# Stick-breaking stage: VectorE in place of ScalarE copies the turned queries and keys out of the score banks

## The chip, the cores and the metric

One core of one Trainium2 chip runs the whole program in one launch. The metric is the device time of that execution in microseconds. Engines are called as in the profile: PE (TensorE), ACT (ScalarE), DVE (VectorE), POOL (GpSimd), SP (SyncE, which here issues the DMAs).

## The reference

One layer of a decoder for a prompt (16 meta rows and 1024 rows) and 64 sample rows. Branch B, for the prompt, is stick-breaking attention over 8 heads of 64:

```python
z = jnp.einsum('bqhd,blhd->bhql', q, k).astype(jnp.float32) * (HEAD_DIM ** -0.5)
strict = (k_pos[None, :] < q_pos[:, None])[None, None]
log_keep = jnp.where(strict, jax.nn.log_sigmoid(-z), 0.0)
after = lax.cumsum(log_keep, axis=3, reverse=True) - log_keep
log_a = jnp.where(strict, jax.nn.log_sigmoid(z) + after, -jnp.inf)
return jnp.einsum('bhql,blhd->bqhd', jnp.exp(log_a).astype(v.dtype), v)
```

The kernel computes it as sigmoid(z) times a running product, from the right, of sigmoid(-z).

## The kernel before, in words

The program is a row of stages with a barrier between them: norm, projections, index scores, the stick-breaking stage (`stick`, the only one that the change touches, about 728 to 908 us of the span), sparse attention, sample attention, merge, FFN, last norm. Each engine's order of work in `stick` is written out by hand; no scheduler moves anything.

`stick` handles four pairs of heads (i = 0 to 3), and for each pair nine tiles of 128 query rows (t = 0 to 8, the last of 16 rows). Tile t sees (t + 1) x 128 keys, 1040 at most, in chunks of 512. The loop variable n (or g) counts tiles over all pairs, 36 in all.

- PE turns the rows of queries and keys of a pair into columns (`turn_qk`, L1095), in five batches: queries and keys of tiles 0 to 3, queries and keys of tiles 4 to 7, and one of tile 8 with both. It scores a chunk for both heads (`score`, L1107) and adds the mask at the diagonal (L1113), turns the weights of tile n - 3 (`turn`, L1125) and multiplies those of tile n - 4 with the values (`use`, L1143).
- ACT takes two sigmoids of each score chunk (`open_tile`, L1189 into `rest`, L1190 into `prob`), copies the turned weights out (`take_turn`, L1198), and the outputs (`evacuate`, L1207). It also copies the turned queries (L1176, with the scale) and keys (L1179): `take_qk`.
- DVE runs one scan over each head of a tile (L1235), once ACT's last sigmoid of that head and tile is there.
- POOL multiplies `prob` with the shifted scan (L1081).

All of turned queries and keys and score chunks go through four PSUM banks in turn. Each use of a bank is a job; job c uses bank c % 4, and PE may write it only when job c - 4 has been read. The jobs around the step from pair 0 to pair 1 are: tile 6 scores 21 to 24 (two chunks, two heads), batches 25 and 26, tile 7 scores 27 to 30, batches 31 and 32, tile 8 scores 33 to 38, batch 39, tile 0 of the next pair 40 and 41. So the second chunk of tile 7 (29, 30) follows batches 25 and 26 in their banks, and the second chunk of tile 8 (35, 36) follows batches 31 and 32. The batches of the next pair are placed by this table:

```python
QK = [("q", 0, 4), ("k", 0, 4), ("q", 4, 4), ("k", 4, 4), ("both", 8, 1)]
QK_WITH = {6: (0, 1), 7: (2, 3), 8: (4,)}
```

The first scores of a pair wait for all five batches of that pair. SP loads the next pair's rows when PE has turned the last batch of this one.

Of the kernel before, what the change touches and what calls it, by code (L numbers as in the profile page):

```python
# [36 lines left out]
ALU = mybir.AluOpType  # L37
ACT = mybir.ActivationFunctionType
AX = mybir.AxisListType

P = 128
# [933 lines left out]
def stick(nc, ctx, proj, ident, q_rows, k_rows, qk_in, selection, sample_mask, load_ahead, out_t):  # L975
# [8 lines left out]
    def sem(name):  # L984
        return nc.alloc_semaphore(f"st_{name}")
# [3 lines left out]
    QK = [("q", 0, 4), ("k", 0, 4), ("q", 4, 4), ("k", 4, 4), ("both", 8, 1)]  # L989
    QK_WITH = {6: (0, 1), 7: (2, 3), 8: (4,)}  # L990
    TURNS = [(g, hh, k0, min(4, g % NT + 1 - k0)) for g in range(NG) for hh in range(2) for k0 in range(0, g % NT + 1, 4)]
    jobs, scores_of, copies_of = 0, [], {}
    for b in range(len(QK)):
        copies_of[0, b] = jobs
        jobs += 1
    for g in range(NG):
        i, t = divmod(g, NT)
        scores_of.append([])
        for a, w in chunks(key_width(t)):
            for hh in range(2):  # L1000
                scores_of[g].append((jobs, hh, a, w))
                jobs += 1
        for b in QK_WITH.get(t, ()) if i + 1 < PAIRS else ():
            copies_of[i + 1, b] = jobs
            jobs += 1
    turns_of = [[c for c, d in enumerate(TURNS) if d[0] == g] for g in range(NG)]

# [15 lines left out]
    mask_made, mask_stored = sem("mask_made"), sem("mask_stored")  # L1023
    v_in = [sem(f"v_in{b}") for b in range(2)]
    stored = [sem(f"stored{b}") for b in range(2)]
    made, taken, scanned, weighed, turns, turns_out, used, o_out = (
        sem(x) for x in ("made", "taken", "scanned", "weighed", "turns", "turns_out", "used", "o_out"))
    tiled = proj.rearrange("(t p) n -> p t n", p=P)

    def half(hh):  # L1030
# [10 lines left out]
    with nc.Block() as block:  # L1041
# [40 lines left out]

        @block.tensor
        def _(pe):
            def turn_qk(i, b):
                what, t0, n = QK[b]
                c = copies_of[i, b]
                if b == 0:
                    pe.wait_ge(qk_in, 32 * (i + 1))
                if c >= NS:  # L1090
                    pe.wait_ge(taken, c - NS + 1)
                for t in range(t0, t0 + n):
                    for k, rows in enumerate([q_rows, k_rows] if what == "both" else [q_rows if what == "q" else k_rows]):
                        at = (t - t0 + k) * P
                        ins = pe.transpose(banks[c % NS][:, at:at + P], rows[:, t, :], ident[:])  # L1095
                ins.then_inc(made, 1)

            def score(g, k):
                i, t = divmod(g, NT)
                r = tile_rows(t)  # L1100
                if t == 0 and k == 0:
                    pe.wait_ge(taken, copies_of[i, len(QK) - 1] + 1)
                last = scores_of[g][-2][0]
                for c, hh, a, w in scores_of[g][2 * k:2 * k + 2]:
                    if hh == 0:
                        pe.wait_ge(taken, c + 1 - NS + 1)
                    ins = pe.matmul(banks[c % NS][:, 0:w], q_t[i % 2][half(hh), t * P:(t + 1) * P],  # L1107
                                    k_t[i % 2][half(hh), a:a + w], start=True, stop=True)
                    if c < last:
                        ins.then_inc(made, 1)  # L1110
                for c, hh, a, w in scores_of[g][2 * k:2 * k + 2] if 2 * k + 2 == len(scores_of[g]) else ():
                    at = slice(t * P - a, t * P - a + r)
                    pe.matmul(banks[c % NS][0:r, at], spread_one[0:r, 0:r], forbidden[0:r, 0:r], start=False, stop=True,  # L1113
                              skip_group_check=True).then_inc(made, 1)

            def turn(c):
                g, hh, k0, n = TURNS[c]
                r = tile_rows(g % NT)
                pe.wait_ge(weighed, 2 * g + hh + 1)
                if c >= NTB:  # L1120
                    pe.wait_ge(turns_out, c - NTB + 1)
                for j in range(n):
                    kt = k0 + j
                    w = tile_rows(kt)
                    ins = pe.transpose(turned[c % NTB][0:w, j, 0:r], prob[g % R][hh][0:r, kt * P:kt * P + w],  # L1125
                                       ident[0:r, 0:r])
                ins.then_inc(turns, 1)

            def use(g):
                i, t = divmod(g, NT)  # L1130
                r = tile_rows(t)
                if t == 0:
                    pe.wait_ge(v_in[i % 2], 16 * (i // 2 + 1))
                pe.wait_ge(turns_out, turns_of[g][-1] + 1)
                b = i * len(O_GROUPS) + group_of[t]
                first, last = O_GROUPS[group_of[t]]
                at = (t - first) * P
                if t == first and b >= 1:
                    pe.wait_ge(o_out, b)
                for kt in range(t + 1):  # L1140
                    w = tile_rows(kt)
                    for hh in range(2):
                        ins = pe.matmul(o[half(hh), at:at + r], v_rows[i % 2][0:w, kt, half(hh)],  # L1143
                                        prob_t[g % 2][hh][0:w, kt, 0:r], start=kt == 0, stop=kt == t,
                                        skip_group_check=True)
                ins.then_inc(used, 1)

            for b in range(len(QK)):
                turn_qk(0, b)
            pe.wait_ge(mask_made, 3)  # L1150
            for n in range(NG + USE_LAG):
                for k, chunks_beside in woven(n):
                    if k is not None:
                        score(n, k)
                    for c in chunks_beside[:NTB]:
                        turn(c)
                    if not k and n >= USE_LAG:
                        use(n - USE_LAG)
                    for c in chunks_beside[NTB:]:
                        turn(c)  # L1160
                if n < NG:
                    i, t = divmod(n, NT)
                    for b in QK_WITH.get(t, ()) if i + 1 < PAIRS else ():
                        turn_qk(i + 1, b)

        @block.scalar
        def _(act):
            def take_qk(i, b):
                what, t0, n = QK[b]
                c = copies_of[i, b]  # L1170
                act.wait_ge(made, c + 1)
                if b == 0 and i >= 2:
                    act.wait_ge(made, scores_of[(i - 1) * NT - 1][-1][0] + 1)
                at = slice(t0 * P, (t0 + n) * P)
                if what in ("q", "both"):
                    ins = act.activation(q_t[i % 2][:, at], banks[c % NS][:, 0:n * P], ACT.Copy, scale=HD ** -0.5)  # L1176
                if what in ("k", "both"):
                    from_k = P if what == "both" else 0
                    ins = act.activation(k_t[i % 2][:, at], banks[c % NS][:, from_k:from_k + n * P], ACT.Copy)  # L1179
                ins.then_inc(taken, 1)  # L1180

            def open_tile(g, k):
                r = tile_rows(g % NT)
                if g >= R and k == 0:
# [21 lines left out]
                w = min(last * P, NP_ROWS) - first * P  # L1206
                act.activation(o_all[i % 2][:, first * P:first * P + w], o[:, 0:w], ACT.Copy).then_inc(o_out, 1)  # L1207

            for b in range(len(QK)):
                take_qk(0, b)  # L1210
            for n in range(NG + USE_LAG):
                for k, chunks_beside in woven(n):
                    if k is not None:
                        open_tile(n, k)
                    for c in chunks_beside:
                        take_turn(c)
                if n >= USE_LAG:
                    i, t = divmod(n - USE_LAG, NT)
                    if t + 1 == O_GROUPS[group_of[t]][1]:
                        evacuate(i, group_of[t])  # L1220
                if n < NG:
                    i, t = divmod(n, NT)
                    for b in QK_WITH.get(t, ()) if i + 1 < PAIRS else ():
                        take_qk(i + 1, b)

        @block.vector
        def _(dve):
            dve.memset(unread[:], 1.0).then_inc(unread_set, 1)
            dve.wait_ge(unread_set, 1)
            for n in range(NG):  # L1230
                r, w = tile_rows(n % NT), key_width(n % NT)
                for hh in range(2):
                    dve.wait_ge(taken, max(c for c, h2, _, _ in scores_of[n] if h2 == hh) + 1)
                    x = rest[n % R][hh][0:r, 0:w]
                    dve.tensor_tensor_scan(x[:, ::-1], x[:, ::-1], unread[0:r, :].to_broadcast([r, w]), 1.0,  # L1235
                                           ALU.mult, ALU.bypass).then_inc(scanned, 1)


def sparse(nc, ctx, proj, ident, q_rows, k_rows, rows_in, selection, out_t, loads):
# [1473 lines left out]
```

## Time and profile before

| | |
|---|---|
| median of 3 runs | 2368.26 us (2366.24 to 2368.83) |
| profiled execution | 2369.87 us, its span 2368.0 us |
| busy over the span | PE 90%, DVE 59%, ACT 32%, POOL 5% |
| mean granted PE clock | 0.959 |

The busy shares are over all stages. In the rows further down a timeline row gives the start, the length, the engine, the line and the operation, what it writes and reads with its shape, how many such instructions it merges (x), and in brackets how long the engine sat idle before it and what released it. An fp32 matmul appears as two records.

### The profile page before, as it was taken

To read this page: it belongs to the slowest core of one execution; us is meant where nothing else is said; L and a number is where in the kernel's file an instruction comes from. 1 tells how busy PE (TensorE), PEld (TensorE's weight loads), DVE (VectorE), ACT (ScalarE), POOL (GpSimd) and SP (SyncE) were. 2 spreads that over 40 slices of the span, in tenths; PEclk is the share of its full clock that TensorE was granted. 3 is DMA by queue.
4 is the path that set the end of the run, shared out by engine and by line. 5 is a ranking of instruction groups with operands and counts; after the bars stand their busy time and mean duration, and the time that the engine had idled before them with its cause. 6 is when DMAs were issued, how large, how long until landed. Compare 5 with 4: busy or idle time off the path is not lost. (4 is left out here: it accounts for less than half of the span.)

```text
span 2368.0 us, 36885 instructions
## 1 busy us (share of the span) xinstructions
PE 2129.3 (90%) x13337; PEld 1768.3 (75%) x13337; DVE 1385.3 (59%) x2428; ACT 764.9 (32%) x1433; POOL 110.3 (5%) x120
## 2 busy tenths in 40 slices
PE   4876999999998987887886989799999999999995
PEld 4832888888885655555555878699999999999994
DVE  5448967665594565573434453345656656656556
ACT  4046011111216896673334331222212122122122
POOL 0000000000004451001000000000000000000000
PEclk7988999999999999998998999899999999999997
DMA  4321222223223102632998440021111011011102
GB/s 152 99 46 45 101 85 85 85 90 114 85 70 94 47 24 65 189 127 81 332 366 316 139 166 27 12 64 54 35 44 53 27 53 53 27 53 36 43 21 89
DMA packets 186052, 218.73 MB, mean 92 GB/s; under 512 B 28828, under 2 KB 119324, under 8 KB 184796
## 3 DMA queue, kind: packets, MB, share of 16 engines
q1 hardware_dynamic: 185300, 217.20, 28.0%
q8 instruction: 65, 1.06, 0.2%
q14 instruction: 39, 0.32, 0.0%
q10 hardware_dynamic: 648, 0.15, 0.0%
HBM read 181.17 MB, written 36.13 MB: 92 GB/s over the span
## 5 line engine op out<-in xcount | busy, mean ns | idle before, releaser
L2447 DVE TENSOR_TENSOR x_all<-x_all,ff_down 128x512 f32<-128x512 f32 x396 | 269.9, 688 | 159.3 <-PE ff_down L2351 159.1
L2336 PE MATMUL ff_up<-m_hi,ff_up_hi 128*128 128x368 f32 x1056 | 348.2, 330 | 8.8 <-DVE ff_up_lo L2424 8.8
L2337 PE MATMUL ff_up<-m_lo,ff_up_hi 128*128 128x368 f32 x1056 | 349.0, 330 | 0.0
L2338 PE MATMUL ff_up<-m_hi,ff_up_lo 128*128 128x368 f32 x1056 | 347.2, 329 | 0.0
L419 PE MATMUL pr_acc<-pr_w_hi,h_hi 128*128 128x512 f32 x720 | 281.0, 390 | 16.3 <-DVE pr_w_lo L356 16.3
L420 PE MATMUL pr_acc<-pr_w_lo,h_hi 128*128 128x512 f32 x720 | 280.7, 390 | 0.0
L421 PE MATMUL pr_acc<-pr_w_hi,h_lo 128*128 128x512 f32 x720 | 280.6, 390 | 0.0
L819 DVE TENSOR_SCALAR_CACHE_REDUCE bi_flags<-scores,bi_thr 128x384 bf16<-128x384 f32 (+6 forms) x231 | 215.9, 993 | 1.2
L2336 PEld LDWEIGHTS ff_up<-m_hi,ff_up_hi 128*128 128x128 f32 x1056 | 198.7, 188 | 10.0 <-DVE ff_up_lo L2424 9.2
L2337 PEld LDWEIGHTS ff_up<-m_lo,ff_up_hi 128*128 128x128 f32 x1056 | 198.7, 188 | 0.8
L2338 PEld LDWEIGHTS ff_up<-m_hi,ff_up_lo 128*128 128x128 f32 x1056 | 198.8, 188 | 0.0
L339 ACT ACTIVATE pr_staged<-pr_acc 128x512 f32<-128x512 f32 x72 | 43.1, 599 | 399.0 <-PE pr_acc L421 399.0
L419 PEld LDWEIGHTS pr_acc<-pr_w_hi,h_hi 128*128 128x128 f32 x720 | 135.6, 188 | 44.6 <-DVE pr_w_lo L356 16.4
L2349 PE MATMUL ff_down<-ff_down_hi,ff_g_hi 128*128 128x512 f32 x396 | 155.1, 392 | 5.8 <-issue 5.8
L421 PEld LDWEIGHTS pr_acc<-pr_w_hi,h_lo 128*128 128x128 f32 x720 | 135.6, 188 | 28.2
L420 PEld LDWEIGHTS pr_acc<-pr_w_lo,h_hi 128*128 128x128 f32 x720 | 135.6, 188 | 28.0
L2351 PE MATMUL ff_down<-ff_down_hi,ff_g_lo 128*128 128x512 f32 x396 | 155.2, 392 | 0.0
L2350 PE MATMUL ff_down<-ff_down_lo,ff_g_hi 128*128 128x512 f32 x396 | 155.1, 392 | 0.0
L1235 DVE TENSOR_TENSOR_SCAN st_rest<-st_rest,st_unread 128x128 f32<-128x128 f32 (+8 forms) x72 | 100.8, 1444 | 67.3 <-ACT st_prob L1190 67.2
L2378 ACT ACTIVATE ff_g_hi<-ff_g 128x1152 fp32r<-128x1152 f32 x22 | 25.7, 1168 | 293.3 <-DVE ff_g L2432 293.3
L356 DVE TENSOR_TENSOR pr_w_lo<-w_raw,pr_w_hi 128x2048 fp32r<-128x2048 f32 x20 | 44.9, 2287 | 119.7 <-ACT pr_w_hi L327 119.7
L1663 PE MATMUL sa_turned<-c_ident,sa_keys 128*128 128x128 f32 x512 | 78.4, 295 | 22.1 <-ACT sa_keys_t L1781 9.1
(274 smaller groups left out, 3575.8 us busy)
## 6 DMA issues: line engine op xcount, KB each, us to landing
out_proj<-pr_staged SPq DMA_DIRECT2D x90, 256.0 KB, 2.0
up_raw<-in_w_up SPq DMA_DIRECT2D x44, 512.0 KB, 5.0
w_raw<-in_w_in SPq DMA_DIRECT2D x10, 2048.0 KB, 8.0
sa_keys<-in_cache_k_a SPq DMA_DIRECT2D x64, 256.0 KB, 4.4
sa_values<-in_cache_v_a SPq DMA_DIRECT2D x64, 256.0 KB, 7.6
sa_keys<-in_cache_k_b SPq DMA_DIRECT2D x64, 256.0 KB, 6.6
sa_values<-in_cache_v_b SPq DMA_DIRECT2D x64, 256.0 KB, 5.4
ff_down_raw<-in_w_down SPq DMA_DIRECT2D x22, 512.0 KB, 3.5
```

Source lines behind the costliest of these rows:

```text
L419: pe.matmul(out, hi[:, c, at], w_hi[s][:, c, 0:width], start=c == 0, stop=False)
L420: pe.matmul(out, hi[:, c, at], w_lo[s][:, c, 0:width], start=False, stop=False)
L421: ins = pe.matmul(out, lo[:, c, at], w_hi[s][:, c, 0:width], start=False, stop=c == KC - 1)
L819: return dve.tensor_scalar(self.flags_of(j), self.of_tile(j), self.thr[:, j:j + 1], None, op, ALU.add, accum_out=self.count[:, j:j + 1])
L1235: dve.tensor_tensor_scan(x[:, ::-1], x[:, ::-1], unread[0:r, :].to_broadcast([r, w]), 1.0, ALU.mult, ALU.bypass).then_inc(scanned, 1)
L2336: pe.matmul(up[n][:], w, hi[:, c, at], start=c == 0, stop=False)
L2337: pe.matmul(up[n][:], w, lo[:, c, at], start=False, stop=False)
L2338: ins = pe.matmul(up[n][:], w_rest, hi[:, c, at], start=False, stop=c == KC - 1)
L2349: pe.matmul(down[n][:], g_hi[:, at], down_hi[:, cols], start=True, stop=False)
L2350: pe.matmul(down[n][:], g_hi[:, at], down_lo[:, cols], start=False, stop=False)
L2351: pe.matmul(down[n][:], g_lo[:, at], down_hi[:, cols], start=False, stop=True).then_inc(down_done, 1)
L2447: dve.tensor_tensor(at, at, down[n][:], ALU.add).then_inc(down_added.sem, 1)
```

## The change

On ACT `take_qk` goes away. DVE gets it: the five batches of pair 0 ahead of everything, and for the next pairs, behind the two scans of tile 6 the first two batches, behind those of tile 7 the next two, behind those of tile 8 the last. Reads of batches are counted on a semaphore of their own (`copied`), reads of score chunks on `taken`; PE waits on the one or the other, by what was in the bank (`in_bank`).

```diff
@@ tables
         for b in QK_WITH.get(t, ()) if i + 1 < PAIRS else ():
             copies_of[i + 1, b] = jobs
+            in_bank.append(("copy", len(QK) * (i + 1) + b))
             jobs += 1
@@ tensor
+            def bank_free(c):
+                if c >= NS:
+                    what, k = in_bank[c - NS]
+                    pe.wait_ge(copied if what == "copy" else taken, k + 1)
...
-                if c >= NS:
-                    pe.wait_ge(taken, c - NS + 1)
+                bank_free(c)
...
-                    pe.wait_ge(taken, copies_of[i, len(QK) - 1] + 1)
+                    pe.wait_ge(copied, len(QK) * (i + 1))
...
-                        pe.wait_ge(taken, c + 1 - NS + 1)
+                        bank_free(c)
+                        bank_free(c + 1)
@@ scalar
-            def take_qk(i, b):
...
-            for b in range(len(QK)):
-                take_qk(0, b)
...
-                if n < NG:
-                    i, t = divmod(n, NT)
-                    for b in QK_WITH.get(t, ()) if i + 1 < PAIRS else ():
-                        take_qk(i + 1, b)
@@ vector
+            def take_qk(i, b):
+                what, t0, n = QK[b]
+                c = copies_of[i, b]
+                dve.wait_ge(made, c + 1)
+                if b == 0 and i >= 2:
+                    dve.wait_ge(made, scores_of[(i - 1) * NT - 1][-1][0] + 1)
+                at = slice(t0 * P, (t0 + n) * P)
+                if what in ("q", "both"):
+                    ins = dve.tensor_scalar(q_t[i % 2][:, at], banks[c % NS][:, 0:n * P], HD ** -0.5, None, ALU.mult)
+                if what in ("k", "both"):
+                    from_k = P if what == "both" else 0
+                    ins = dve.tensor_copy(k_t[i % 2][:, at], banks[c % NS][:, from_k:from_k + n * P])
+                ins.then_inc(copied, 1)
+
+            for b in range(len(QK)):
+                take_qk(0, b)
             dve.memset(unread[:], 1.0).then_inc(unread_set, 1)
...
                     dve.tensor_tensor_scan(x[:, ::-1], x[:, ::-1], unread[0:r, :].to_broadcast([r, w]), 1.0,
                                            ALU.mult, ALU.bypass).then_inc(scanned, 1)
+                i, t = divmod(n, NT)
+                for b in QK_WITH.get(t, ()) if i + 1 < PAIRS else ():
+                    take_qk(i + 1, b)
```

DVE, from tile 6's second scan to the next pair's tile 0, before (the scans are listed under the name SCALAR_TENSOR_TENSOR; `st_rest_0` and `_1` are the two heads):

```order
L1235 SCALAR_TENSOR_TENSOR st_rest_1<-st_rest_1,st_unread 128x896
L1235 SCALAR_TENSOR_TENSOR st_rest_0<-st_rest_0,st_unread 128x1024
L1235 SCALAR_TENSOR_TENSOR st_rest_1<-st_rest_1,st_unread 128x1024
L1235 SCALAR_TENSOR_TENSOR st_rest_0<-st_rest_0,st_unread 16x1040
L1235 SCALAR_TENSOR_TENSOR st_rest_1<-st_rest_1,st_unread 16x1040
L1235 SCALAR_TENSOR_TENSOR st_rest_0<-st_rest_0,st_unread 128x128
```

and now:

```order
L1239 SCALAR_TENSOR_TENSOR st_rest_1<-st_rest_1,st_unread 128x896
L1224 TENSOR_SCALAR st_q_t<-st_banks 128x512
L1227 COPY st_k_t<-st_banks 128x512
L1239 SCALAR_TENSOR_TENSOR st_rest_0<-st_rest_0,st_unread 128x1024
L1239 SCALAR_TENSOR_TENSOR st_rest_1<-st_rest_1,st_unread 128x1024
L1224 TENSOR_SCALAR st_q_t<-st_banks 128x512
L1227 COPY st_k_t<-st_banks 128x512
L1239 SCALAR_TENSOR_TENSOR st_rest_0<-st_rest_0,st_unread 16x1040
L1239 SCALAR_TENSOR_TENSOR st_rest_1<-st_rest_1,st_unread 16x1040
L1224 TENSOR_SCALAR st_q_t<-st_banks 128x128
L1227 COPY st_k_t<-st_banks 128x128
L1239 SCALAR_TENSOR_TENSOR st_rest_0<-st_rest_0,st_unread 128x128
```

Six instructions came in per pair, two behind each pair of scans of tiles 6, 7 and 8.

ACT, from tile 6's last sigmoid to tile 7's first, before:

```order
L1190 ACTIVATE st_prob_1<-st_banks 128x384
L1198 ACTIVATE st_prob_t_1<-st_turned 128x512
L1176 ACTIVATE st_q_t<-st_banks 128x512
L1179 ACTIVATE st_k_t<-st_banks 128x512
L1189 ACTIVATE st_rest_0<-st_banks 128x512
L1190 ACTIVATE st_prob_0<-st_banks 128x512
```

and now:

```order
L1184 ACTIVATE st_prob_1<-st_banks 128x384
L1192 ACTIVATE st_prob_t_1<-st_turned 128x512
L1183 ACTIVATE st_rest_0<-st_banks 128x512
L1184 ACTIVATE st_prob_0<-st_banks 128x512
L1183 ACTIVATE st_rest_1<-st_banks 128x512
```

The two copies left; nothing else moved on ACT, and PE's instructions stand in the same order as before.

## Rows read from the trace of the kernel before

**Rows 1.** The page: its header, and the busy time of each engine.

```profile
span 2368.0 us, 36885 instructions
PE 2129.3 (90%) x13337; PEld 1768.3 (75%) x13337; DVE 1385.3 (59%) x2428; ACT 764.9 (32%) x1433; POOL 110.3 (5%) x120
```

**Rows 2.** Window of one pair: us, PE, PEld, DVE, ACT, POOL busy, PEclk, DMA, GB/s.

```profile
765.00:810.00 45.00, 40.67 (x375) 27.17 (x376) 26.49 (x19) 37.34 (x103) 23.14 (x18) 0.96 0.20 53
```

**Rows 3.** Waits of the stage, 728 to 915 us: total, times, longest.

```profile
DVE st_rest L1235 <- ACT st_prob L1190: 67.2, 31, 6.0
...
PE st_banks L1107 <- ACT st_k_t L1179: 2.7, 4, 0.9
```

**Rows 4.** Timeline of ACT, stage's start and step from pair 0 to 1.

```profile
732.77 1.28 ACT L1189 ACT_TABLE_LOAD   x1
...
751.74 0.86 ACT L1179 ACTIVATE st_k_t<-st_banks 128x512 f32<-128x512 f32 x1
752.42 0.67 ACT L1189 ACTIVATE st_rest<-st_banks 128x512 f32<-128x512 f32 x1
...
756.74 0.62 ACT L1190 ACTIVATE st_prob<-st_banks 128x512 f32<-128x512 f32 x1
...
758.80 0.69 ACT L1179 ACTIVATE st_k_t<-st_banks 128x512 f32<-128x512 f32 x1
759.28 0.57 ACT L1189 ACTIVATE st_rest<-st_banks 16x512 f32<-16x512 f32 x1
...
764.82 0.25 ACT L1176 ACTIVATE st_q_t<-st_banks 128x128 f32<-128x128 f32 x1
764.98 0.26 ACT L1179 ACTIVATE st_k_t<-st_banks 128x128 f32<-128x128 f32 x1
```

**Rows 5.** Timeline of PE: the scores of tiles 7, 8, 0 and 1.

```profile
751.18 1.13 PE L1107 MATMUL st_banks<-st_k_t,st_q_t 64*128 64x512 f32 x4 [0.73 <-ACT st_prob L1190]
...
753.96 1.13 PE L1107 MATMUL st_banks<-st_k_t,st_q_t 64*128 64x512 f32 x4
...
757.41 1.13 PE L1107 MATMUL st_banks<-st_k_t,st_q_t 64*128 64x512 f32 x4 [0.60 <-ACT st_prob L1190]
...
760.30 1.13 PE L1107 MATMUL st_banks<-st_k_t,st_q_t 64*128 64x512 f32 x4
...
765.29 0.77 PE L1107 MATMUL st_banks<-st_k_t,st_q_t 64*128 64x128 f32 x4 [0.59 <-ACT st_k_t L1179]
...
770.63 0.70 PE L1107 MATMUL st_banks<-st_k_t,st_q_t 64*128 64x256 f32 x4
```

**Rows 6.** Timeline of DVE: scans of tiles 6, 7, 8, and the last tile.

```profile
750.40 3.93 DVE L1235 TENSOR_TENSOR_SCAN st_rest<-st_rest,st_unread 128x896 f32<-128x896 f32 x2 [0.76 <-ACT st_prob L1190]
756.41 4.46 DVE L1235 TENSOR_TENSOR_SCAN st_rest<-st_rest,st_unread 128x1024 f32<-128x1024 f32 x2 [2.08 <-ACT st_prob L1190]
764.08 5.14 DVE L1235 TENSOR_TENSOR_SCAN st_rest<-st_rest,st_unread 16x1040 f32<-16x1040 f32 x4 [3.21 <-ACT st_prob L1190]
...
892.23 4.52 DVE L1235 TENSOR_TENSOR_SCAN st_rest<-st_rest,st_unread 16x1040 f32<-16x1040 f32 x2 [2.62 <-ACT st_prob L1190]
```

**Rows 7.** Groups by line and shape on DVE: count, busy us, mean ns.

```profile
L1863 DVE COPY sa_keys_t<-sa_turned 128x512 f32<-128x512 f32 x64 | 44.2, 690 | 54.7 <-PE sa_turned L1663 54.7
...
L1432 DVE COPY sp_o_all<-sp_o 128x128 f32<-128x128 f32 x32 | 9.1, 285 | 20.8 <-PE sp_o L1361 20.8
...
L1461 DVE TENSOR_SCALAR sp_prob<-sp_prob,sp_part 128x512 f32<-128x512 f32 x8 | 3.5, 484 | 0.1
```

**Rows 8.** Windows behind the first and third step; PE's timeline at the third.

```profile
765.20:767.00 1.80, 1.71 (x10) 1.49 (x11) 1.80 (x2) 0.63 (x5) 0.53 (x1) 0.54 0.55 134
...
854.00:856.00 2.00, 2.00 (x30) 1.66 (x29) 2.00 (x1) 1.19 (x4) 1.96 (x1) 1.00 0.00 0
...
852.76 0.49 PE L1107 MATMUL st_banks<-st_k_t,st_q_t 64*128 64x128 f32 x4 [0.59 <-ACT st_k_t L1179]
...
856.55 0.70 PE L1107 MATMUL st_banks<-st_k_t,st_q_t 64*128 64x256 f32 x4
```

More of the change, by code:

```diff
@@ L991, in stick @@
     TURNS = [(g, hh, k0, min(4, g % NT + 1 - k0)) for g in range(NG) for hh in range(2) for k0 in range(0, g % NT + 1, 4)]
-    jobs, scores_of, copies_of = 0, [], {}
+    jobs, scores_of, copies_of, in_bank = 0, [], {}, []
     for b in range(len(QK)):
         copies_of[0, b] = jobs
+        in_bank.append(("copy", b))
         jobs += 1
@@ L1001, in stick @@
                 scores_of[g].append((jobs, hh, a, w))
+                in_bank.append(("score", sum(what == "score" for what, _ in in_bank)))
                 jobs += 1
@@ L1025, in stick @@
     stored = [sem(f"stored{b}") for b in range(2)]
-    made, taken, scanned, weighed, turns, turns_out, used, o_out = (
-        sem(x) for x in ("made", "taken", "scanned", "weighed", "turns", "turns_out", "used", "o_out"))
+    made, taken, copied, scanned, weighed, turns, turns_out, used, o_out = (
+        sem(x) for x in ("made", "taken", "copied", "scanned", "weighed", "turns", "turns_out", "used", "o_out"))
     tiled = proj.rearrange("(t p) n -> p t n", p=P)
@@ L1167, in _ @@
         def _(act):
-            def take_qk(i, b):
[L1169 to L1180, printed above, removed]
             def open_tile(g, k):
@@ L1232, in _ @@
                 for hh in range(2):
-                    dve.wait_ge(taken, max(c for c, h2, _, _ in scores_of[n] if h2 == hh) + 1)
+                    dve.wait_ge(taken, in_bank[max(c for c, h2, _, _ in scores_of[n] if h2 == hh)][1] + 1)
                     x = rest[n % R][hh][0:r, 0:w]
```

## The prediction

> **What bounds the kernel now.** I read the page first. Its header and busy line [rows 1] say that PE is the busiest engine of the whole program (90%) and that ACT is busy 32%. Neither number says what the stick stage pays, so I went to that stage. A window over one of its four head pairs [rows 2] shows PE and ACT nearly equally busy (40.67 and 37.34 of 45 us), DVE at 26.49, POOL at 23.14. The waits of the stage [rows 3] show DVE waiting 67.2 us for ACT's sigmoids in 31 waits: DVE has gaps, but it is fed late. So the order in time decides, and I followed the step from pair 0 to pair 1 on ACT, PE and DVE [rows 4 to 6]. Three such steps exist, 43.7 us apart (half of 765.29 to 852.76) [rows 5, 8], and look alike.
>
> The reader is to see three things in them. First, PE, not ACT, is what the first chunk of tile 7 waits for: ACT starts its last copy of tile 6 at 751.74, and the next sigmoid starts at 752.42, 0.68 us later, where full-width instructions of a backlog follow each other every 0.48 (758.80 to 759.28) [rows 4]. PE could begin these scores only at 751.18, when ACT had read tile 6's last sigmoid [rows 5]. The two copies of tile 6 thus lie in time in which ACT would have little else. Second, PE starts the second chunk of tile 7 at 753.96, of tile 8 at 760.30, and the first tile of the next pair at 765.29 [rows 5]; the last comes right behind ACT's last copy, which begins at 764.98 [rows 4]. The row of waits names these copies too [rows 3]. Third, DVE's scans run far behind: tile 6's two take from 750.40 to 754.33, tile 7's from 756.41 to 760.87, and tile 8's begin at 764.08 [rows 6], when ACT's copies are nearly through.
>
> **The change, part by part.** Per step ACT loses four copies of 128x512 and two of 128x128. At its backlog pitch that is 4 x 0.48 + 2 x 0.16 (764.82 to 764.98) [rows 4] = 2.2 us of ACT. DVE gets the same six, each set behind both scans of its tile. Their price is not shown for DVE in this stage; the nearest rows are DVE's copies out of PSUM in a later one, 0.69 us at 128x512 and 0.285 at 128x128 [rows 7]. The lower bound for a full one is the 0.48 us of a multiply by a scalar out of SBUF [rows 7]. I take 0.69, since operation, memory and shape are the same, and count 1.35 for a pair of them, which overlap by some 0.03.
>
> First the rows, then a rule: 0.69 us for 512 columns and 0.285 for 128 make 1.05 ns a column. The Trainium skill ("VectorE: DVE Perf Modes", the perf-mode tier table) allows a copy or a multiply that touches PSUM up to twice that rate; by the table's cycle formula I estimate 0.4 us for each, and the sum below would shrink by 4 x 0.29 = 1.2 us per step. The row decides.
>
> Now the chain, in the clock of the trace of before.
> (a) Tile 6. The scans end at 754.33 [rows 6]; the two copies end at 754.33 + 1.35 = 755.68. The second chunk of tile 7 goes into exactly the two banks that they read, so PE starts it at 755.7 and not at 753.96: **+1.75**. Behind it on PE stand the turns of tile 4 and the next transposes; ACT gets the chunk 1.75 later, and would have had no work left to hide it, by the first point above.
> (b) Tile 7. Its last sigmoid ends at 757.36 (756.74 + 0.62) [rows 4], now 759.1; the first chunk of tile 8 starts on PE at 759.15, not 757.41. DVE's scans move from 756.41 to 758.15 and end 4.46 later [rows 6], at 762.6; the copies end at 763.97. PE's second chunk of tile 8 stands at their banks: 764.0, not 760.30: **+3.7 in all**. ACT is no limit there: it has the first chunk at about 760.4 (PE's 759.15 plus 1.1 for the scores and 0.2 for the signal), is through at 762.4, and idles.
> (c) Tile 8. Its scans start at 764.08 + 3.7 = 767.8 and take 4.52 (the pair alone in the last head pair) [rows 6]: 772.3. The two small copies end at 772.85. The scores of the next pair's tile 0 need all its queries and keys, so PE starts them at 772.9, not 765.29: **+7.6**. They are the first thing in PE's queue; behind them are the turns of tile 6 and the products of tile 5, which are ready and must wait too.
> Is it absorbed afterwards? From 765.29 to 770.63 and on, PE runs dense [rows 5]: 40.67 of 45 us in the pair's window [rows 2]. A shift of PE's start there is a shift of everything. POOL's products of tile 8 move with the scans, and PE turns them only behind the first scores of the next pair's tile 2. The remaining tiles of a pair have no copy behind their scans and keep their pace. So three steps cost 3 x 7.6 = 22.8 us.
>
> The start of the stage: ACT's table load of 1.28 us stands behind its copies at 732.77 and holds the first sigmoid until it ends at 734.05 [rows 4]. ACT has no copies now and can load at once; DVE's ten copies' worth of columns end about 0.3 us later than ACT's. The two cancel to within 0.2 us: nought, and what covers it is that exchange.
>
> The clock: in the first step PE's granted clock is 0.54 (1.2 GHz) from 765.2 to 767.0, behind a wait of 0.59 us [rows 5]; in the third, behind the same wait of 0.59, it is 1.00 (2.4 GHz) [rows 8]. From tile 0's scores to tile 1's the first step takes 5.34 us, the third 3.79 (852.76 to 856.55) [rows 5, 8]: a dip costs 1.5 us. With PE idle for some 4.7 us ahead of each tile 0, I expect the dip at all three steps, so +1.5 at the third. That PE's clock falls back when it idles is also what the Trainium skill says ("TensorE: Matmul & The Clock Gate", HAM oscillation); the trace agrees at the first step and not at the third.
>
> **Sum:** 22.8 + 1.5 = +24.3 us. The profiled execution took 2369.87 us, with a span of 2368.0; the median is 2368.26, lower by 0.07%. On the median: **2392.5**.
>
> **Rivals.**
> *The early delays are absorbed.* If the +3.7 of (a) and (b) ended in slack, only (c) would be left: scans from 764.08 to 768.6, copies to 769.15, PE from 765.29 to 769.2, +3.9 a step, +11.7 in all, **2380.0**. For it: ACT is rid of 2.2 us. Against: the chunks stand on banks that only DVE empties.
> *ACT was the bound, and the stage gets faster.* The 2.2 us per step come straight off ACT's line: 3 x 2.2 = -6.6, **2361.7**. It decides if DVE is done with its copies before PE asks for the bank, that is, if the scans of tile 6 and their copies end by 753.96; the rows say 755.68. For it speaks that ACT is busy for 37.34 of the 45 us [rows 2]. The Trainium skill speaks on this side as well ("TensorEngine Tiling (Array Packing)", PSUM Bottleneck): use both ScalarE and VectorE to empty PSUM. Here DVE already has its scans in front.
> *The clock falls more often.* PE gets new waits of about 1.5 us at tile 7 and 2 us at tile 8 besides the long one. A dip of 1.5 us at each of these six as well is +9, **2401.5**. Against: the same short wait ahead of tile 0 brought one at the first step and none at the third.
> *Nothing moves.* The copies could turn out not to be on any path, if the stage waited for something else throughout: **2368**. The waits name the copies, so hardly.
>
> **How the numbers follow.** A measurement of this kernel tells about 0.2% (4.7 us) from no change. Forecast 0.75, absorbed 0.11, faster 0.04, clock 0.08, nothing 0.02. The bounds of a copy (0.48 to 0.69) take up to 0.8 us a step off, 2390; a smaller overlap or a dip less or more moves it by 3 more; with the absorbed case at the low end and part of the clock case at the high end the range is 2380 to 2400. Faster 0.04, same 0.03, slower 0.93.
>
> **What would show it.** In the profile after: DVE's scan pairs of tiles 6 to 8 followed without a gap by copies of 0.69, 0.69 and 0.28 us; PE waiting for DVE ahead of the second chunks of tiles 7 and 8 and, some 4.7 us long, ahead of tile 0; the head pairs 51 us apart instead of 43.7; the last pair as long as before; low clock after each long wait. It is wrong if tile 0 of pair 1 starts less than 5 us later against the stage's start, if the copies take 0.4 us, or if PE has gained back part of the shift by tile 3.

## The result, and the profile after

The changed kernel is slower: a ratio of 1.0119 to the kernel before, 95% interval 1.0103 to 1.0136, with medians of 2399.83 us (2394.05 to 2404.57, 4 runs) and 2368.55 us. The profiled execution took 2394.05 us, 24.2 more than that of before (2369.87). The forecast was 2392.5 on the median, with 2380 to 2400; the measured median lies 0.2 us inside the upper end.

DVE's timeline at the first of the three steps between head pairs, which answers to [rows 6]; start us, length us, and in brackets the idle time before:

```profile
750.61 3.93 DVE L1239 TENSOR_TENSOR_SCAN st_rest<-st_rest,st_unread 128x896 f32<-128x896 f32 x2 [0.76 <-ACT st_prob L1184]
754.45 0.67 DVE L1224 TENSOR_SCALAR st_q_t<-st_banks 128x512 f32<-128x512 f32 x1
755.03 0.68 DVE L1227 COPY st_k_t<-st_banks 128x512 f32<-128x512 f32 x1
758.31 4.46 DVE L1239 TENSOR_TENSOR_SCAN st_rest<-st_rest,st_unread 128x1024 f32<-128x1024 f32 x2 [2.59 <-ACT st_prob L1184]
762.69 0.67 DVE L1224 TENSOR_SCALAR st_q_t<-st_banks 128x512 f32<-128x512 f32 x1
763.27 0.68 DVE L1227 COPY st_k_t<-st_banks 128x512 f32<-128x512 f32 x1
767.67 4.52 DVE L1239 TENSOR_TENSOR_SCAN st_rest<-st_rest,st_unread 16x1040 f32<-16x1040 f32 x2 [3.72 <-ACT st_prob L1184]
772.12 0.25 DVE L1224 TENSOR_SCALAR st_q_t<-st_banks 128x128 f32<-128x128 f32 x1
772.30 0.27 DVE L1227 COPY st_k_t<-st_banks 128x128 f32<-128x128 f32 x1
```

Each pair of copies starts right behind its scans. PE's timeline of the same stretch, against [rows 5]:

```profile
751.48 1.13 PE L1115 MATMUL st_banks<-st_k_t,st_q_t 64*128 64x512 f32 x4 [0.82 <-ACT st_prob L1184]
...
755.86 1.13 PE L1115 MATMUL st_banks<-st_k_t,st_q_t 64*128 64x512 f32 x4 [1.53 <-DVE st_k_t L1227]
...
759.40 1.13 PE L1115 MATMUL st_banks<-st_k_t,st_q_t 64*128 64x512 f32 x4 [0.77 <-ACT st_prob L1184]
...
764.10 1.13 PE L1115 MATMUL st_banks<-st_k_t,st_q_t 64*128 64x512 f32 x4 [1.74 <-DVE st_k_t L1227]
...
772.63 0.80 PE L1115 MATMUL st_banks<-st_k_t,st_q_t 64*128 64x128 f32 x4 [3.88 <-DVE st_k_t L1227]
...
777.89 0.70 PE L1115 MATMUL st_banks<-st_k_t,st_q_t 64*128 64x256 f32 x4
```

Three waits for DVE's copies stand where there were no waits or one of 0.59 us for ACT. The waits of the stage, in all, against [rows 3] (total, times, longest): a new one of 22.6 us, of which 21.5 are these three waits at three steps and 1.1 one at the stage's start; and ACT idles for PE.

```profile
DVE st_rest L1239 <- ACT st_prob L1184: 77.3, 34, 4.8
ACT st_rest L1183 <- PE st_banks L1121: 28.4, 16, 5.0
...
PE st_banks L1115 <- DVE st_k_t L1227: 22.6, 10, 3.9
```

To compare kernels I measure the stage from the scans of pair 0's tile 5, ahead of the first moved copy, to those of the last tile. First two rows of before, then three of after:

```profile
746.24 3.40 DVE L1235 TENSOR_TENSOR_SCAN st_rest<-st_rest,st_unread 128x768 f32<-128x768 f32 x2 [0.81 <-ACT st_prob L1190]
789.95 3.40 DVE L1235 TENSOR_TENSOR_SCAN st_rest<-st_rest,st_unread 128x768 f32<-128x768 f32 x2 [0.81 <-ACT st_prob L1190]
```

```profile
746.45 3.40 DVE L1239 TENSOR_TENSOR_SCAN st_rest<-st_rest,st_unread 128x768 f32<-128x768 f32 x2 [0.88 <-ACT st_prob L1184]
797.30 3.40 DVE L1239 TENSOR_TENSOR_SCAN st_rest<-st_rest,st_unread 128x768 f32<-128x768 f32 x2 [0.88 <-ACT st_prob L1184]
...
915.74 4.52 DVE L1239 TENSOR_TENSOR_SCAN st_rest<-st_rest,st_unread 16x1040 f32<-16x1040 f32 x2 [2.62 <-ACT st_prob L1184]
```

From 746.24 to 892.23 [rows 6] that is 145.99 us before, and from 746.45 to 915.74 it is 169.29 after: **+23.3**. By pair the distances are 43.71, 43.77 and 42.21 before, 50.85, 51.02 and 51.11 after.

This start can mislead, because TensorE's clock is low at the head of the stage too, and not for the same time in every execution. PE's first transposes of the stage, and a window behind them (columns as in [rows 2]), in the kernel before:

```profile
728.50 3.47 PE L1095 MATMUL st_banks<-c_ident,w_raw 128*128 128x128 f32 x18 [4.15 <-PEq L2567]
732.00:738.00 6.00, 4.53 (x28) 2.14 (x30) 3.08 (x6) 5.91 (x18) 2.05 (x5) 1.00 1.19 301
```

and in a second execution of the same kernel:

```profile
728.33 4.07 PE L1095 MATMUL st_banks<-c_ident,w_raw 128*128 128x128 f32 x18 [4.14 <-PEq L2567]
732.00:738.00 6.00, 5.36 (x22) 2.37 (x22) 2.00 (x4) 4.73 (x14) 1.73 (x4) 0.52 1.17 299
```

From the first transpose to the tile 5 scans the first took 17.74 us, the second 19.39; and the second then had no low clock at its first step, where it was 1.57 us shorter. So the table gives both measures to the last tile's scans: from PE's first transpose, and from the tile 5 scans of pair 0. By the first the change costs 23.2 us. Ratios are to the kernel before, run beside it.

| kernel | from the first transpose, us | from tile 5's scans, us | pair to pair, us | ratio, 95% interval |
|---|---|---|---|---|
| before | 163.73 | 145.99 | 43.71, 43.77, 42.21 | |
| before, again | 163.82 | 144.43 | 42.14, 43.77, 42.21 | 0.9997, 0.9988 to 1.0006 |
| the change | 186.93 | 169.29 | 50.85, 51.02, 51.11 | 1.0119, 1.0103 to 1.0136 |
| the change, again | 187.01 | 169.36 | 50.89, 51.04, 51.12 | 1.0105, 1.0086 to 1.0123 |
| copies ahead of the scans | 163.80 | 146.16 | 43.78, 43.85, 42.22 | 1.0009, 0.9998 to 1.0019 |
| only tile 8's behind | 176.69 | 159.05 | 47.44, 47.61, 47.70 | 1.0059, 1.0041 to 1.0076 |
| only tiles 6 and 7's behind | 176.74 | 157.13 | 45.61, 47.53, 47.68 | 1.0060, 1.0042 to 1.0077 |
| between the two scans | 172.16 | 154.51 | 46.30, 45.34, 46.57 | 1.0038, 1.0023 to 1.0053 |
| the change, PE kept busy | 186.60 | 166.99 | 49.39, 50.47, 50.82 | 1.0095, 1.0076 to 1.0113 |
| ACT copies, last batch early | 165.43 | 147.69 | 42.73, 44.30, 44.35 | 1.0016, 1.0005 to 1.0027 |
| DVE ahead, last batch early | 159.73 | 140.12 | 41.26, 41.27, 41.28 | 0.9998, 0.9987 to 1.0008 |
| the same, again | 159.71 | 140.10 | 41.27, 41.26, 41.26 | 0.9999, 0.9990 to 1.0009 |
| DVE ahead, batches spread | 160.06 | 140.71 | 41.76, 41.74, 40.91 | 0.9991, 0.9979 to 1.0002 |

### The profile page after: what moved, and what is told of

Its sections match the earlier page's. It is cut to its first block and busy times, and to the rows that moved or that the text cites. A ratio compares the mean times of both kernels' runs of the same rounds, so it can differ in the third digit from the quotient of the medians.

```text
span 2392.0 us, 36942 instructions
## 1 busy us (share of the span) xinstructions
PE 2135.0 (89%) x13337; PEld 1773.1 (74%) x13337; DVE 1397.3 (58%) x2452; ACT 758.1 (32%) x1409; POOL 110.4 (5%) x120
## 5 line engine op out<-in xcount | busy, mean ns | idle before, releaser
L421 PEld LDWEIGHTS pr_acc<-pr_w_hi,h_lo 128*128 128x128 f32 x720 | 135.6, 188 | 28.2
L1084 POOL TENSOR_TENSOR st_prob<-st_prob,st_rest 128x127 f32<-128x127 f32 (+8 forms) x72 | 92.7, 1293 | 99.0 <-DVE st_rest L1239 97.7
```

The source lines that it names most:

```text
L421: ins = pe.matmul(out, lo[:, c, at], w_hi[s][:, c, 0:width], start=False, stop=c == KC - 1)
```

## The experiments

**The place in DVE's queue, or DVE itself.** All copies stay on DVE, but each batch goes ahead of its tile's scans.

```diff
+            EARLY = (6, 7, 8)
...
+                i, t = divmod(n, NT)
+                for b in QK_WITH.get(t, ()) if t in EARLY and i + 1 < PAIRS else ():
+                    take_qk(i + 1, b)
                 for hh in range(2):
...
-                for b in QK_WITH.get(t, ()) if i + 1 < PAIRS else ():
+                for b in QK_WITH.get(t, ()) if t not in EARLY and i + 1 < PAIRS else ():
                     take_qk(i + 1, b)
```

> The changed kernel, but VectorE takes each batch ahead of the two scans of its tile, not behind them. Theory Q (queue: the cost is that the copies stand behind 4 to 4.5 us of scans in VectorE's queue): the banks are empty as early as with ScalarE, the stage is 3 us shorter than in the kernel before, since ScalarE is rid of 2.2 us per step of which a third to a half was in PE's way: ratio about 0.999 to 1.000 of the kernel before. Theory E (engine: VectorE's copy and its signal are slower than ScalarE's): 0.09 us per copy or more stays, and the kernel is 1 to 3 us slower than before. Theory B (the scans, now later, become the wait): tile 0 of the next pair waits on POOL's products, 1 us a step or more.

The stage took 146.16 us, 0.2 more than before (0.1 from the first transpose); the ratio is 1.0009 with 1 in its interval. So DVE as such costs nothing that shows, and the loss of 23 us in the stage comes from the place behind the scans. Theory B fails too: the scans are later, and PE has no wait for POOL's products at the step. But theory Q's gain did not come either. PE's timeline shows why:

```profile
754.55 1.13 PE L1115 MATMUL st_banks<-st_k_t,st_q_t 64*128 64x512 f32 x4
...
758.09 1.13 PE L1115 MATMUL st_banks<-st_k_t,st_q_t 64*128 64x512 f32 x4 [0.76 <-ACT st_prob L1184]
...
764.57 0.41 PE L1133 MATMUL st_turned<-c_ident,st_prob 128*128 128x128 f32 x2 [1.05 <-ACT st_prob_t L1192]
...
765.77 0.61 PE L1115 MATMUL st_banks<-st_k_t,st_q_t 64*128 64x128 f32 x4 [0.58 <-DVE st_k_t L1227]
```

The second chunk of tile 7 has no wait again, and ahead of the next pair's tile 0 PE waits 0.58 us for DVE's copy where it waited 0.59 for ACT's [rows 5]. Whoever copies, the last batch is turned right ahead of the scores that need it, and that wait stays. Most of ACT's freed 2.2 us is spent waiting for PE: between the first scores of tile 7 and those of tile 0 its waits add up to 2.9 us, where before there was one of 1.17.

**Which copies.** Only tile 8's two small copies stay behind the scans: the same edit with `EARLY = (6, 7)`.

> Batches of tiles 6 and 7 ahead of the scans, only the two small copies of tile 8 behind them. By the prediction's part (c) each step costs +3.9 us, three steps 11.7, and a low clock of 1.5 us at the third step besides: about +12 to +13 us over the kernel before. If the step's cost comes from the full-width copies instead, it is near 0.

Stage +13.1 (+13.0 from the first transpose), at the upper end of what part (c) gives. At each step PE waits 4.34 us for 0.25 and 0.27 us of copies; here the first step, with two windows in its wait:

```profile
767.63 0.80 PE L1115 MATMUL st_banks<-st_k_t,st_q_t 64*128 64x128 f32 x4 [4.34 <-DVE st_k_t L1227]
...
763.00:764.00 1.00, 0.28 (x3) 0.04 (x1) 1.00 (x1) 0.51 (x2) 0.00 (x0) 1.00 0.00 0
764.00:768.00 4.00, 0.37 (x2) 0.38 (x4) 3.57 (x4) 0.00 (x0) 2.74 (x2) 0.50 0.96 247
```

PE's clock falls inside this wait, at all three steps.

The other half: `EARLY = (8,)`, so tiles 6 and 7's batches stay behind.

> Batches of tiles 6 and 7 behind the scans, that of tile 8 ahead. By parts (a) and (b) PE's second chunk of tile 8 starts 3.7 us later at each step, and nothing is added behind it: about +11 us over the kernel before. If the early delays are absorbed by ScalarE's freed time (the rival), it is under +3.

The stage is 11.1 us longer from tile 5's scans, which is the forecast, and 13.0 from the first transpose. The match of the first number is in part luck: this execution had its low clock at the head of the stage and not at the first step. The delay itself is read from the second step, where both kernels had low clock: 47.53 us against 43.77, +3.76, as worked out from (a) and (b). The early delays are passed on, not absorbed, and that closes the first rival. From the first transpose the two halves add up to 26.0 us, the change to 23.2; each half has one low stretch more than before (some 1.65 us), which comes only once in the sum. The 1.1 us left stay open.

**How deep in the queue.** The batch goes between the two scans.

```diff
+                i, t = divmod(n, NT)
                 for hh in range(2):
...
                                            ALU.mult, ALU.bypass).then_inc(scanned, 1)
-                i, t = divmod(n, NT)
-                for b in QK_WITH.get(t, ()) if i + 1 < PAIRS else ():
-                    take_qk(i + 1, b)
+                    for b in QK_WITH.get(t, ()) if hh == 0 and i + 1 < PAIRS else ():
+                        take_qk(i + 1, b)
```

> The changed kernel with each batch between the two scans of its tile (behind one scan of 2.0 to 2.3 us, not two). By theory Q (the copies cost what they stand behind) and the rows of before: tile 6's copies end at 753.7, tile 7's at 760.0, both before PE wants the banks (753.96, 760.30), so nothing there; tile 8's end at 766.9 where PE started tile 0 at 765.29: +1.6 us a step, +5 in all, up to +8 with low clock behind the wait. If the cost were proportional to the scans ahead, half of the +23: +12.

Stage +8.5 (+8.4 from the first transpose), a little over the upper end of 5 to 8 and well under 12. The second step is 1.57 us longer than before, as worked out; at the first and third the low clock adds to it (at the first, tile 0's scores to tile 1's take 6.31 us, against 5.34 before). The copies of tiles 6 and 7 are done before PE asks; those of tile 8 are not. DVE's timeline:

```profile
753.05 0.68 DVE L1227 COPY st_k_t<-st_banks 128x512 f32<-128x512 f32 x1
...
759.42 0.68 DVE L1227 COPY st_k_t<-st_banks 128x512 f32<-128x512 f32 x1
...
764.21 2.31 DVE L1240 TENSOR_TENSOR_SCAN st_rest<-st_rest,st_unread 16x1040 f32<-16x1040 f32 x1 [1.92 <-ACT st_prob L1184]
766.45 0.25 DVE L1224 TENSOR_SCALAR st_q_t<-st_banks 128x128 f32<-128x128 f32 x1
```

The cost is not in proportion to the scans ahead; it is the time by which a copy misses PE's need for the bank.

**The clock.** PE turns the identity 30 times into the bank that tile 0's scores then overwrite, where it would wait; this work is not used.

```diff
+                    if i > 0:
+                        c = scores_of[g][0][0]
+                        bank_free(c)
+                        for _ in range(30):
+                            pe.transpose(banks[c % NS][:, 0:P], ident[:], ident[:])
                     pe.wait_ge(copied, len(QK) * (i + 1))
```

> The changed kernel with 30 transposes of the identity on PE, into the bank that tile 0's first scores then overwrite, ahead of its wait for the copies (some 4 us of work in which PE waits anyway). It adds work that is not used. Theory C (clock: part of the cost is PE at 1.2 GHz behind the long wait): the granted clock stays at 1.00 behind the wait, and from tile 0's scores to tile 1's take 3.8 us instead of 5.3: 3 to 5 us faster than the changed kernel, so about +20 to +25 over before. If the clock costs nothing here: the same as the changed kernel or slower.

From the first transpose the stage is 0.3 to 0.4 us shorter than in the change's two executions, against 3 to 5 expected; the ratio, 1.0095, lies below 1.0105 and 1.0119, with intervals that overlap. (From tile 5's scans it is 2.3 us shorter, but 2.0 of these were spent ahead of them, where the clock was low for long in this execution.) Windows of the change at its first step (us, then busy time of PE, PEld, DVE, ACT, POOL, the granted clock, DMA):

```profile
764.00:766.00 2.00, 1.90 (x11) 0.96 (x12) 0.00 (x0) 0.77 (x2) 0.85 (x1) 0.92 0.00 0
766.00:768.00 2.00, 1.56 (x10) 1.15 (x9) 0.33 (x1) 2.00 (x9) 0.00 (x0) 0.50 0.00 0
...
774.00:776.00 2.00, 2.00 (x14) 1.67 (x14) 0.76 (x2) 1.62 (x6) 1.06 (x3) 0.52 0.08 18
```

And with the filler, its 30 transposes at the first step, then windows and PE's timeline at the second:

```profile
768.39 3.44 PE L1113 MATMUL st_banks<-c_ident 128*128 128x128 f32 x30
...
816.00:818.00 2.00, 1.72 (x8) 1.34 (x9) 0.66 (x1) 1.91 (x8) 0.00 (x0) 0.50 0.00 0
...
822.00:824.00 2.00, 2.00 (x21) 1.71 (x20) 0.24 (x2) 0.00 (x0) 1.95 (x1) 1.00 1.07 260
...
818.20 5.25 PE L1113 MATMUL st_banks<-c_ident 128*128 128x128 f32 x30
823.38 0.49 PE L1120 MATMUL st_banks<-st_k_t,st_q_t 64*128 64x128 f32 x4
```

At the first step the clock stays at 2.4 GHz, tile 0's scores to tile 1's take 3.78 us (772.90 to 776.68) instead of 5.26 with the change, and the pair is 1.46 us shorter. That prices a low clock, but it can't be credited to the filler: in the change the clock had fallen in tile 8, ahead of the place where the filler stands. At the second and third step the clock had fallen to 1.2 GHz in tile 8 here as well. The filler brought it back for the scores, but at 1.2 GHz its transposes took 5.25 and 5.61 us instead of 3.44 and ran past the moment at which the copies were there: from tile 8's second chunk to tile 0 PE took 9.62 and 9.98 us, where the change took 8.53. That ate most of the gain; these pairs are 0.55 and 0.29 us shorter. So this run doesn't measure what the clock costs in all. The traces do: three steps of the change have low clock, at some 1.5 us each, and two of before have it too, so that about 1.6 of the 23.2 us are clock and the rest are waits.

**The change itself again.**

> The changed kernel itself once more, in more rounds. In the stage its trace is 23.3 us longer than before; its median was 28 to 31 us up in four runs. If the stage is the whole effect, the median difference is 23 to 26 us; if something else comes in, it stays at 28 or more.

The stage repeats to 0.1 us (169.36). The median is 2398.75, about 27 us over the runs beside it. The ratio, 1.0105, is 24.9 us, and its interval, 20 to 29 us, holds the stage's 23.2; the first comparison (1.0119, 24 to 32 us) lies just above it. So the stage may be the whole effect, and that something else comes in is not shown.

**The kernel before, unchanged, again.**

> The kernel before, with a profile of its own. The stage is set by its order and by how many of the three steps see a low clock: from pair 0's tile 5 scans to the last tile's, 143 to 147 us (146.0 in the first trace, two steps of three with low clock). The stages behind it show how much one execution differs from another without any change: if the sparse stage's PE clock alone moves the whole by 2 us or more, the 3 to 5 us by which the changed kernel's median exceeds its stage's loss need no cause of their own.

The stage took 144.43 us from tile 5's scans, and only one step had the low clock; but from PE's first transpose it took 163.82, against 163.73. What the first step saved had been spent at the head of the stage. From the last tile's scans to the end of the span before took 1475.8 us (892.23 to 2368.0), and this unchanged kernel 1478.8 (892.15 to 2370.9); the change took 1476.3, and again 1479.6. A spread of 3 us behind the stage is there without any change.

**Can DVE's copies pay?** The wait of 0.58 us stays because tile 8's batch is turned last. The table was changed first with the copies on ACT, then with those of DVE ahead of the scans.

```diff
-    QK_WITH = {6: (0, 1), 7: (2, 3), 8: (4,)}
+    QK_WITH = {6: (0, 1), 7: (2, 3, 4)}
```

> The kernel before (copies on ScalarE), with the last batch (tile 8's queries and keys) turned with tile 7's and not behind tile 8. Theory P (PE's chain at the end of a pair is the bound: it waits 0.59 us for the last copy ahead of the next tile 0): 0.6 to 1.2 us a step gained, 2 to 3.5 us in all, 0.9990. If ScalarE is the bound of that stretch, nothing.

> Both: copies on VectorE ahead of the scans of tiles 6 and 7, the last batch with tile 7's. By theory P as the run with ScalarE's copies, 2 to 3.5 us faster than before; if ScalarE's freed time is worth something once PE no longer waits for a copy, 1 us a step more.

On ACT it was a miss: stage 147.69, ratio 1.0016. The wait ahead of tile 0 is gone, but a larger one has come ahead of tile 8, where the third batch shifts the banks, so that one of tile 8's first two jobs (34 and 35) follows a batch (31) and not a score chunk, and ACT gets to that batch only behind tile 7's sigmoids:

```profile
758.59 1.13 PE L1107 MATMUL st_banks<-st_k_t,st_q_t 64*128 64x512 f32 x4 [2.02 <-ACT st_q_t L1176]
...
765.40 0.49 PE L1107 MATMUL st_banks<-st_k_t,st_q_t 64*128 64x128 f32 x4
```

On DVE, which takes the batch as soon as it is turned, both waits are small, and no step sees a low clock:

```profile
759.48 1.13 PE L1115 MATMUL st_banks<-st_k_t,st_q_t 64*128 64x512 f32 x4 [0.46 <-ACT st_prob L1184]
...
766.29 0.49 PE L1115 MATMUL st_banks<-st_k_t,st_q_t 64*128 64x128 f32 x4
```

From the first transpose the stage is 159.73 us, 4.0 shorter than before and 5.7 shorter than the same table on ACT (from tile 5's scans 4.3 to 5.9 and 7.6, in part because the low clock lay ahead of them). A pair without low clock takes 41.27 us, against 42.2 before and 42.73 with the same table on ACT: 0.9 a pair, 2.8 in all, is PE's shorter chain, as theory P has it. The rest is low clock, of which there was 2.0 us more at the head of the stage and none at the steps, where before had it at two. Here, and only here, it matters which engine copies; whether that is because ACT is free or because DVE takes the batch at once, these runs don't separate. The whole, however, came out at 0.9998. So I ran it again, and a version with the batches spread (`QK_WITH = {4: (0,), 5: (1,), 6: (2,), 7: (3, 4)}`, all ahead of the scans).

> Copies on VectorE ahead of the scans, last batch with tile 7's, once more. Theory P: the stage is 140 us again (41.3 a pair, no low clock), 3 to 6 us shorter than the kernel before, and the whole 2 to 5 us faster. If the second look gives the same median as before again, the gain in the stage is lost behind it.

> As that, but the batches spread over tiles 4, 5, 6 (one each) and 7 (two), each in a wait of PE for ScalarE of 0.5 to 0.8 us, copied by VectorE ahead of the tile's scans. If PE is the bound of tiles 6 to 8, a pair takes up to 1 us less than 41.3; if ScalarE's pace bounds tiles 4 to 6, where every bank is in use, each extra bank use costs there instead and the pair is as long or longer.

The stage repeats at 140.10 (159.71 from the first transpose), and the whole at 0.9999: the 2 to 5 us expected in the whole did not come, and where they went is not shown. The spread version's batches of tiles 4 and 5 lie ahead of tile 5's scans in pair 0, so only the first transpose is a fair start: 160.06, no shorter, although its clock was low for 3 us at the head of the stage and not for 9. That is as expected if ACT's pace counts in tiles 4 to 6, which no run tests by itself. Its ratio of 0.9991 is the lowest, with 1 inside its interval. None of these beats the kernel before by what can be measured in the whole; the gain is shown for the stage alone.

## Why the prediction was right

The forecast named the direction, the mechanism and the range. The delays came where it put them, each a little smaller. That the median is inside the range is close to luck: 2399.83 against an upper end of 2400, which had been set for a low clock at more places, and that is not what brought it there.

- *(a), predicted +1.75.* From the first chunk of tile 7 to its second: 2.78 us before (751.18 to 753.96) [rows 5], 4.38 after (751.48 to 755.86): +1.60.
- *(b), predicted +3.7 in all.* To tile 8's second chunk 9.12 before, 12.62 after: +3.50.
- *(c), predicted +7.6 in all.* To tile 0: 14.11 before, 21.15 after: +7.04. PE's wait ahead of tile 0 is 3.88 us, not 4.7. All three are a little high. For (a) and (b) the reason is that a pair of full-width copies takes 1.26 us (754.45 to 755.71), not 1.35, since they start 0.58 us apart. In (c) two more things come in: tile 8's scans move by 3.29 us and not by 3.7, as ACT had a small backlog there before (its sigmoids of the second chunk began 1.36 us behind PE's start, now 1.13), and the two small copies take 0.45 us together, not 0.55. The row [rows 7] gave the right length of a full-width copy. The Trainium skill ("VectorE: DVE Perf Modes", the perf-mode tier table) lists these operations with up to 2x on PSUM, and the estimate of 0.4 us came from that; but the same page limits fp32 with a PSUM operand to 1x (Why PSUM operands drop a tier), and the trace agrees with that: 0.67 to 0.69 us each, no doubled rate.
- *No absorption.* The pairs follow each other 7.1 and 7.3 us later, the size of the shift at tile 0; the run with only tiles 6 and 7's copies behind shows it for its part (+3.76 at the second step). The last pair, which moves no copies, is as long as before (16.31 us from tile 5's scans to tile 8's, against 16.30).
- *The clock, predicted +1.5 at the third step.* The third pair is 8.90 us longer, 1.65 more than the second. But in the change the low clock begins in tile 8, ahead of the long wait that I named. The two halves of the change tell the two apart, and each has low clock at the third step, where before had none: with tile 8's copies alone behind (no waits for DVE at tiles 7 and 8) the clock falls in the long wait, at all three steps; with only tiles 6 and 7's behind (and 0.58 us of wait ahead of tile 0) it falls in tile 8 at the second and third step. The price was right, the place was not.
- *The start, predicted nought.* From PE's first transpose (728.50, now 728.81) the tile 5 scans come at 17.74 us before and 17.64 after. (In the second execution of before it is 19.39, with the clock low for longer.)
- *The sum, predicted +24.3.* The stage gives +23.3 and the profiled execution +24.2. The medians give +31 and +27, the ratios 28.2 and 24.9 us. What was too small there is the last step, from one profiled execution to the median: it assumed that the rest of the program takes the same time. With a spread of 3 us behind the stage between two executions of an unchanged kernel, and 23.2 inside the interval of the second comparison, a part of the gap needs no cause of its own; whether the later stages take longer on the average behind the changed one is not settled.
- *The rivals.* That ACT was the bound is refuted by the copies ahead of the scans (no shorter, with ACT rid of the same work). For the advice to empty PSUM with both engines ("TensorEngine Tiling (Array Packing)" in the Trainium skill, PSUM Bottleneck), the runs say that for this stage it paid only with the copies ahead of the scans and PE's order changed as well: 159.7 us from the first transpose, against 165.4 with the same order on ACT and 163.7 before.

## What to carry to other kernels

When work is moved to an engine with idle time, ask not how much is idle but what stands ahead of the moved instruction in that engine's queue, and when its consumer needs it: here, with tile 8's alone behind, half a microsecond of copies behind 4.5 us of scans made PE wait for 4.3 us. A buffer that several kinds of work share in turn passes such a delay on to work that has nothing to do with it, so list which job follows which in each bank. A freed engine gains nothing until the chain through the bounding engine is shortened too, and a gain of a few microseconds in one stage may not be seen in the whole. When a stage is measured from trace to trace, start the measure where the stage starts: a start in its middle made a low clock that had only moved look like a gain of 1.6 us.

## What the hardware showed beyond that

PE's clock can be low in different places in two executions of the same kernel, at nearly the same total. Before, the first step took 43.71 us in one and 42.14 in the other, with the third step at 42.21 in both; but at the head of the stage the granted clock was low until about 731 us in the one and until about 738 us in the other, and from the first transpose both took 163.7 to 163.8 us. The same goes for all thirteen traces: in the five with low clock for some 9 us at the head, the clock was 1.00 throughout at the first step, in kernels with waits (only tiles 6 and 7's behind, and the filler) and without; in six of the eight with some 3 us of it, it fell at the first step. No run shows why.

With the change all three steps had low clock. In the three traces of the versions with DVE's copies ahead and the last batch early or spread none had: the granted clock was 1.00 behind each of nine steps.
